# Up projection of a two-level (fp32 as high and low parts) encoder layer: activations' high and low parts side by side for 512 wide matmuls, and the last sum of weight quadrants by an accumulating DMA

## The chip, the cores and the metric

One core of a Trainium2 chip. The metric is the device time of one execution in microseconds (us), the median of three runs.

## The reference

One encoder layer on x of 512 tokens by 2048 channels, float32: a combined input projection, two token mixers, a merge, an output projection, a first layer norm, then the feed forward part and a second layer norm. The change touches the first product of the feed forward part:

```python
def conv_glu(x, w_up, conv_w, conv_b, w_down):
    u = x @ w_up                       # 512 x 2048 by 2048 x 11008
    gate, val = jnp.split(u, 2, axis=-1)
    a = jax.nn.gelu(dwconv_centred(gate, conv_w, conv_b), approximate=False)
    return (a * val) @ w_down
```

The convolution is over tokens, three taps per channel.

## The kernel before

Float32 accuracy is made from reduced-precision passes: each operand is split into a high part (rounded by ScalarE, `hi`) and the low rest (VectorE, `operand - high`), and a product is high by high, high by low and low by high, three matmuls that add up in the same PSUM bank.

The up projection runs in 43 steps (`FB`). A step makes 128 gate channels and the 128 val channels that go with them, for all 512 tokens, by Strassen's scheme in Winograd's form: the weight columns and rows make four quadrants of 1024 by 128 (gate or val columns, upper or lower half of the 2048 rows), the activations four of 1024 by 256 tokens, and seven products of 1024 by 128 by 256 replace eight. A step is therefore seven **blocks** (i = 0 to 6); `OPS` and `BANK` say which activation operand and which PSUM bank a block uses. The seven activation operands are made once, split, and stay in `aop`. A block is 8 slices of the contraction (`up_block`, L2267), each three matmuls of 256 columns by `add_three` (L2222): weight high by activation high (L2223), weight high by activation low (L2224), weight low by activation high (L2225).

Weights. SyncE loads the four quadrants of a step into `quad` (two sets, so a step ahead; L479, four transfers of 512 KB), each when the quadrant of two steps before has been split for the last time. Blocks 0, 3 and 5 use quadrants as loaded; the others use sums: block 1 takes q12 + q11, made by an accumulating DMA of GpSimd that adds q11's bytes from HBM to the loaded q12 (`add_b11`, L651, counted by `t1_in`); block 2 takes that + q22 (`form(step, 1)`, VectorE, L1528); block 4 takes q11 - that (`form(step, 2)`, L1532); block 6 takes block 2's sum + q21 (`form(step, 3)`, L1535). Each operand is then split: `operand_hi` (ScalarE, L989), which waits until the block three before is done, since `uw` has three buffers, and `operand_lo` (VectorE, L1553). The block waits for `op_lo`.

Results of a step. Between the blocks ScalarE copies PSUM banks: `seed` (L1070; bank of block 0 into the bank of blocks 2, 4, 6), `p5_copy` (L1075), `u2_copy` (L1080), and `gate_half` twice (L1093 copies the gate, L1094 makes the middle tap of the convolution with its bias). VectorE makes `c22` (L1721) and `c12` (L1726), each 128 x 256 from a PSUM bank and a copy, the outer taps in `conv` (L1731, L1732), and `product` (L1746) after ScalarE's `gelu` (L1099). Block 6 waits for `c22_done`, because `c22` frees the bank that it writes. All these act on [128, 256] halves of the tokens, or on [128, 512].

Every second step two products are combined and split for the down projection (`sums`, `ah_hi`, `ah_lo` L1758) and SyncE stores them with one transfer of 1792 KB (`spill`, L484) behind the four quadrant loads of that step. In 32 of the steps GpSimd also stores one chunk of the layer norm's output and loads the next (`store_chunk` L670, `load_chunk` L664); VectorE scales it in two parts (`residual`, L1772 in slot i = 3 and L1775 in slot i = 6).

Every engine's order is written out by hand: for each step and each i a fixed list (ScalarE from L1114, VectorE from L1777, GpSimd from L672, TensorE from L2281). An engine that waits holds up everything behind it. On GpSimd the order per step is: wait for a scaled chunk, store it, wait for the store, load the next chunk, wait for a loaded q12, `add_b11`.

"Step" below is one of the 43, "block" one of its seven products.

## Time and profile before

| | |
|---|---|
| three runs | 2813.02, 2815.32, 2814.93 us; median 2814.93 |
| the profiled execution's own time | 2812.55 us |
| its span, first to last instruction | 2810.5 us |
| mean granted TensorE clock | 0.988 |
| busy share of the span: TensorE, its weight loads, VectorE, ScalarE, GpSimd | 97%, 86%, 66%, 45%, 8% |
| first and last weight load of the up projection's matmuls | 1477.3 us, 2361.7 us |

A busy time sums durations of instructions; matmuls are pipelined, so their durations overlap and the distance between two starts is what a matmul costs in a dense stretch. "To landing" is from a DMA's issue to its last completion. A timeline row has start, duration, engine, line, and in brackets the idle time before it and what ended that.

### The profile page before, as it was taken

The page shows a single profiled execution, that of the slowest core. Times are in us where ns is not written, and L with a number is a line of the kernel's source. Part 1 is how long each engine was busy: PE and PEld are TensorE (multiplying, and loading weights), DVE is VectorE, ACT ScalarE, POOL GpSimd, SP SyncE. Part 2 cuts the span into 40 slices and gives each one's busy share as a digit, 9 for nine tenths or more (in the row PEclk, how much of TensorE's full clock was granted, in tenths as well). Part 3 has the DMA queues.
Part 4 walks back from the last instruction along what each step waited for, and adds up shares of the span by engine and source line. Part 5 has one row for each costly group of instructions (what it writes and reads, how often), then busy time and mean ns, then how long its engine had stood idle before and what let it go on. Part 6 is the DMA issues. An engine that isn't in the chain of part 4 may idle for free.

```text
span 2810.5 us, 42096 instructions
## 1 busy us (share of the span) xinstructions
PE 2737.0 (97%) x15963; PEld 2418.1 (86%) x15963; DVE 1844.4 (66%) x2452; ACT 1256.2 (45%) x1833; POOL 227.8 (8%) x298
## 2 busy tenths in 40 slices
PE   8999999999999999999979999999999999999995
PEld 7788888888888888888868999999999999888884
DVE  4465454555443333337897888888888876778788
ACT  4444444443333222224455555555555554444444
POOL 2000001110100000001010111111111101000000
PEclk9999999999999999999989999999999999999998
DMA  4333333332334444448535677767776768357452
GB/s 153 94 88 85 90 90 95 80 88 74 90 86 124 123 139 130 123 123 329 196 112 137 187 174 204 196 179 191 205 187 172 193 183 325 144 206 262 157 184 87
DMA packets 473748, 427.37 MB, mean 152 GB/s; under 512 B 16008, under 2 KB 417724, under 8 KB 469376
## 3 DMA queue, kind: packets, MB, share of 16 engines
q1 hardware_dynamic: 400672, 302.03, 35.1%
q0 software_dynamic: 70144, 119.04, 16.2%
q10 hardware_dynamic: 2784, 4.26, 0.4%
q8 instruction: 101, 1.65, 0.2%
q14 instruction: 47, 0.39, 0.0%
HBM read 361.28 MB, written 64.01 MB: 151 GB/s over the span
## 4 chain that ended last, share of the span: by engine, by line
PE 88%; DVE 8%; DMA 2%; issue 1%; ACT 1%; ACTq 0%; DVEq 0%
PE ps L2223 15%; PE ps L2224 14%; PE ps L2225 14%; PE ps L1961 14%; PE ps L1963 14%; PE ps L1962 14%; PE ps L1955 1%; DVE uw L1553 1%; PE ps L2171 1%; ACT uw L989 1%; DMA racc<-h_dram 1%; DVE aop L1706 1%; PE ps L2151 0%; DMA x_tok<-in_x 0%; DMA hx<-hn_dram 0%
## 5 line engine op out<-in xcount | busy, mean ns | idle before, releaser
L1185 DVE TENSOR_TENSOR wlo<-raw,whi 128x512 fp32r<-128x512 f32 x416 | 286.6, 691 | 629.2 <-ACT whi L724 626.3
L2223 PE MATMUL ps<-aop,uw 128*128 128x256 f32 x2408 | 685.1, 285 | 9.2 <-DVE aop L1706 6.2
L2224 PE MATMUL ps<-aop,uw 128*128 128x256 f32 x2408 | 683.1, 284 | 0.0
L2225 PE MATMUL ps<-aop,uw 128*128 128x256 f32 x2408 | 682.9, 284 | 0.0
L724 ACT ACTIVATE whi<-raw 128x512 fp32r<-128x512 f32 x416 | 260.7, 630 | 729.3 <-PE ps L1963 728.6
L1961 PE MATMUL ps<-xt_hi,whi 128*128 128x512 f32 x1408 | 553.2, 393 | 1.7 <-DVE wlo L1185 1.7
L1963 PE MATMUL ps<-xt_hi,wlo 128*128 128x512 f32 x1408 | 549.2, 390 | 0.0
L1962 PE MATMUL ps<-xt_lo,whi 128*128 128x512 f32 x1408 | 548.8, 390 | 0.0
L2223 PEld LDWEIGHTS ps<-aop,uw 128*128 128x128 f32 x2408 | 463.9, 193 | 13.0 <-DVE aop L1706 6.9
L2224 PEld LDWEIGHTS ps<-aop,uw 128*128 128x128 f32 x2408 | 464.0, 193 | 0.0
L2225 PEld LDWEIGHTS ps<-aop,uw 128*128 128x128 f32 x2408 | 463.9, 193 | 0.0
L1553 DVE TENSOR_TENSOR uw<-quad,uw 128x1024 fp32r<-128x1024 f32 x301 | 367.6, 1221 | 141.1 <-ACT uw L989 140.1
L989 ACT ACTIVATE uw<-quad 128x1024 fp32r<-128x1024 f32 x301 | 318.1, 1057 | 231.2 <-DVE quad L1535 138.9
L1961 PEld LDWEIGHTS ps<-xt_hi,whi 128*128 128x128 f32 x1408 | 264.7, 188 | 57.7 <-DVE wlo L1185 2.1
L1963 PEld LDWEIGHTS ps<-xt_hi,wlo 128*128 128x128 f32 x1408 | 264.6, 188 | 55.7
L1962 PEld LDWEIGHTS ps<-xt_lo,whi 128*128 128x128 f32 x1408 | 264.8, 188 | 53.3
L989 ACT ACTIVATE dw<-region 128x1024 fp32r<-128x1024 f32 x168 | 154.3, 919 | 218.1 <-PE ps L2225 202.8
L1553 DVE TENSOR_TENSOR dw<-region,dw 128x1024 fp32r<-128x1024 f32 x168 | 173.0, 1042 | 72.0 <-ACT dw L989 71.9
L2223 PE MATMUL ps<-dw,aopb 128*128 128x512 f32 x560 | 218.0, 389 | 1.7 <-DVE dw L1553 1.2
L2224 PE MATMUL ps<-dw,aopb 128*128 128x512 f32 x560 | 217.9, 389 | 0.0
L2225 PE MATMUL ps<-dw,aopb 128*128 128x512 f32 x560 | 217.8, 389 | 0.0
L2223 PEld LDWEIGHTS ps<-dw,aopb 128*128 128x128 f32 x560 | 105.1, 188 | 24.3 <-DVE dw L1553 1.6
(287 smaller groups left out, 3455.5 us busy)
## 6 DMA issues: line engine op xcount, KB each, us to landing
raw<-in_w_in SPq DMA_DIRECT2D x352, 256.0 KB, 2.7
quad<-in_ffn_w_up SPq DMA_DIRECT2D x172, 512.0 KB, 3.9
region<-in_ffn_w_down SPq DMA_DIRECT2D x32, 1280.0 KB, 9.1
a_dram<-ah SPq DMA_DIRECT2D x20, 1792.0 KB, 9.6
aopb<-a_dram POOLq DMA_DIRECT2D x28, 1280.0 KB, 8.1
quad<-in_ffn_w_up POOLq DMA_DIRECT2D x43, 512.0 KB, 6.6
w_region<-in_w_out SPq DMA_DIRECT2D x16, 1024.0 KB, 8.0
m_dram<-mh POOLq DMA_DIRECT2D x8, 1792.0 KB, 6.8
```

The lines of the kernel that those rows point to most:

```text
L724: nc.scalar.activation(whi[:, k % HL, :], raw[:, k % RAW, :], ACT.Copy).then_inc(w_hi_ready, 1)
L989: nc.scalar.activation(dst, src, ACT.Copy).then_inc(s["op_hi"], 1)
L1185: nc.vector.tensor_tensor(wlo[:, k % HL, :], raw[:, k % RAW, :], whi[:, k % HL, :].bitcast(F32), ALU.subtract).then_inc(w_lo_ready, 1)
L1553: nc.vector.tensor_tensor(w[:, 1, :, :], src, w[:, 0, :, :].bitcast(F32), ALU.subtract).then_inc(s["op_lo"], 1)
L1706: nc.vector.tensor_tensor(aop[:, :, 1, k, :], hs[k % 3][:, 0:7, :], aop[:, :, 0, k, :].bitcast(F32), ALU.subtract).then_inc(s["a_lo_done"], 1)
L1955: return nc.tensor.transpose(o, i, ident[0:rows, 0:rows])
L1961: mm(o, a_hi, b_hi, start=first, stop=False)
L1962: mm(o, a_hi, b_lo, start=False, stop=False)
L1963: return mm(o, a_lo, b_hi, start=False, stop=last)
L2223: mm(o, a_hi, b_hi, start=first, stop=False, skip_group_check=True)
L2224: mm(o, a_hi, b_lo, start=False, stop=False, skip_group_check=True)
L2225: return mm(o, a_lo, b_hi, start=False, stop=last, skip_group_check=True)
```

## The change

Three things. In `aop` the high and low parts of each slice stand side by side, and `up_block` multiplies the weight's high part by both in one matmul of 512 columns, then (before it, except in the first slice) the weight's low part by the high part in one of 256. The columns 0 to 255 of a bank then hold two of the three terms and 256 to 511 the third, so every PSUM operation works on 512 columns instead of 256, and the two halves are added at the end: `gate_low`, `gate_sum`, `conv_middle` replace `gate_half`, and `val_sum` adds up what `c22` and `c12` leave in the wider `p5c` and `u2c`. Third, `form(step, 3)` is gone: GpSimd adds q21 to `quad[...][1]` by a second accumulating DMA (`add_b21`), issued after block 2's operand is split and `form(step, 2)` is done, behind the next step's `add_b11` in GpSimd's order. `form(step, 2)` moves from slot i = 3 to slot i = 2. Left out below: two places where the counts of `p5_added` in the down projection shift.

```diff
@@ -88,7 +88,7 @@
 T_W = 8 * W_STEPS
-T_UP = T_W + 3 * FB
+T_UP = T_W + 2 * FB
@@ -230,14 +230,14 @@
         uw = sb("uw", [P, 3, 2, 8, P], 0, F32R)
-        aop = sb("aop", [P, 7, 2, 8, 256], 32 * K, F32R)
+        aop = sb("aop", [P, 7, 8, 2, 256], 32 * K, F32R)
         hs = [sb(f"hs{n}", [P, 8, 256], at * K) for n, at in enumerate((24, 160, 8))]
...
         ft = sb("ft", [P, S], 198 * K)
-        p5c = sb("p5c", [P, 256], 200 * K)
-        u2c = sb("u2c", [P, 256], 201 * K + 512)
+        p5u2 = sb("p5u2", [P, 1920], 200 * K)
+        p5c, u2c = p5u2[:, 0:512], p5u2[:, 1408:1920]
@@ -326,6 +326,11 @@
             return sum(r in held for held in REGIONS[:step + 1])
+        def p5u2_part(part):
+            head = p5u2[:, 256 * part:256 * part + 1]
+            return bass.AP(head.tensor, head.offset + 1408, [list(head.ap[0]), [-1408, 2], [1, 256]])
@@ -651,6 +656,13 @@
+            def add_b21(step):
+                pool.wait_ge(s["op_lo"], N_W + 7 * step + 3)
+                pool.wait_ge(s["t_formed"], T_W + 2 * step + 2)
+                pool.dma_start(quad[step % 2][1][:, :, :], wup[:, 8:16, step * P:(step + 1) * P],
+                               accum_op=ALU.add).then_inc(t1_in[step % 2], 16)
@@ -672,15 +684,20 @@
             load_chunk(0)
-            for step in range(2, 5):
-                add_b11(step)
+            for step in range(4):
+                if step:
+                    add_b11(step + 1)
+                add_b21(step)
             for c in range(32):
...
                 add_b11(c + 5)
+                add_b21(c + 4)
             for step in range(37, FB):
                 add_b11(step)
+                add_b21(step - 1)
+            add_b21(FB - 1)
@@ -957,10 +974,10 @@
                     else:
-                        if i == 1:
-                            act.wait_ge(t1_in[step % 2], 16 * (step // 2 + 1))
+                        if i in (1, 6):
+                            act.wait_ge(t1_in[step % 2], 16 * (2 * (step // 2) + 1 + (i == 6)))
                         else:
-                            act.wait_ge(s["t_formed"], T_W + 3 * step + {2: 1, 4: 2, 6: 3}[i])
+                            act.wait_ge(s["t_formed"], T_W + 2 * step + i // 2)
@@ -1004,7 +1021,7 @@
                 act.wait_ge(s["s_formed"], 8 + k + 1)
-                nc.scalar.activation(aop[:, :, 0, k, :], hs[k % 3][:, 0:7, :], ACT.Copy).then_inc(s["a_hi_done"], 1)
+                nc.scalar.activation(aop[:, :, k, 0, :], hs[k % 3][:, 0:7, :], ACT.Copy).then_inc(s["a_hi_done"], 1)
@@ -1065,34 +1082,39 @@
                 if step >= 2:
-                    act.wait_ge(s["c22_done"], W_STEPS + step - 1)
+                    act.wait_ge(s["c21_done"], W_STEPS + step - 1)
                 b0 = 3 * (step % 2)
-                nc.scalar.activation(ps[:, b0 + 1, 0:256], ps[:, b0, 0:256], ACT.Copy).then_inc(s["seed_done"], 1)
+                nc.scalar.activation(ps[:, b0 + 1, :], ps[:, b0, :], ACT.Copy).then_inc(s["seed_done"], 1)
             def p5_copy(step):
                 act.wait_ge(s["op_used"], N_W + 7 * step + 2)
-                act.wait_ge(s["c22_done"], W_STEPS + step)
-                nc.scalar.activation(p5c[:, :], ps[:, 3 * (step % 2) + 2, 0:256], ACT.Copy).then_inc(s["p5_copied"], 1)
+                act.wait_ge(s["p5_added"], W_STEPS + step)
+                if step == 0:
+                    act.wait_ge(s["ht_ps"], KB)
+                nc.scalar.activation(p5c, ps[:, 3 * (step % 2) + 2, :], ACT.Copy).then_inc(s["p5_copied"], 1)
             def u2_copy(step):
                 act.wait_ge(s["op_used"], N_W + 7 * step + 3)
-                act.wait_ge(s["c12_done"], W_STEPS + step)
-                nc.scalar.activation(u2c[:, :], ps[:, 3 * (step % 2) + 1, 0:256], ACT.Copy).then_inc(s["u2_copied"], 1)
-            def gate_half(step, half):
-                bank = 3 * (step % 2) + half
-                ts = slice(256 * half, 256 * half + 256)
-                if half == 0:
-                    act.wait_ge(s["op_used"], N_W + 7 * step + 4)
-                    if step == 0:
-                        act.wait_ge(s["hn_out"], 16 * 8)
+                act.wait_ge(s["p5_added"], W_STEPS + step)
+                nc.scalar.activation(u2c, ps[:, 3 * (step % 2) + 1, :], ACT.Copy).then_inc(s["u2_copied"], 1)
+            def gate_low(step):
+                act.wait_ge(s["op_used"], N_W + 7 * step + 7)
+                act.wait_ge(s["conv_done"], step)
+                b0 = 3 * (step % 2)
+                nc.scalar.activation(gate[:, :].rearrange("p (a t) -> p a t", a=2), ps[:, b0:b0 + 2, 256:512],
+                                     ACT.Copy).then_inc(s["c11_done"], 1)
+            def conv_middle(step):
+                act.wait_ge(s["c21_done"], W_STEPS + step + 1)
+                if step == 0:
+                    act.wait_ge(s["hn_out"], 16 * 8)
+                else:
                     act.wait_ge(s["mul_done"], step)
-                else:
-                    act.wait_ge(s["op_used"], N_W + 7 * step + 7)
-                nc.scalar.activation(gate[:, ts], ps[:, bank, 0:256], ACT.Copy)
-                nc.scalar.activation(ft[:, ts], ps[:, bank, 0:256], ACT.Identity, scale=par[:, PAR_FW + FB + step:PAR_FW + FB + step + 1],
-                                     bias=par[:, PAR_FB + step:PAR_FB + step + 1]).then_inc(s[("c11_done", "c21_done")[half]], 1)
+                nc.scalar.activation(ft[:, :], gate[:, :], ACT.Identity, scale=par[:, PAR_FW + FB + step:PAR_FW + FB + step + 1],
+                                     bias=par[:, PAR_FB + step:PAR_FB + step + 1]).then_inc(s["conv_a"], 1)
@@ -1120,21 +1142,22 @@
                     if i == 2 and step:
-                        gate_half(step - 1, 1)
+                        gate_low(step - 1)
                     if 7 * step + i >= 3:
                         operand_hi(N_W + 7 * step + i)
-                    if i == 3 and step:
+                    if i == 2 and step:
+                        conv_middle(step - 1)
+                    if i == 4 and step:
                         gelu(step - 1)
                     if i == 1 and step >= 3 and step % 2 and step < LEFT + 2:
                         ah_hi((step - 3) // 2)
-                    if i == 6:
-                        gate_half(step, 0)
                     if step == FB - 1 and i >= 5:
...
             operand_hi(N_UP + 1)
-            gate_half(FB - 1, 1)
+            gate_low(FB - 1)
             operand_hi(N_UP + 2)
+            conv_middle(FB - 1)
...
@@ -1524,15 +1547,12 @@
                     quad_ready(step, 3)
-                    dve.wait_ge(t1_in[step % 2], 16 * (step // 2 + 1))
+                    dve.wait_ge(t1_in[step % 2], 16 * (2 * (step // 2) + 1))
                     ins = nc.vector.tensor_tensor(q12[:, :, :], q12[:, :, :], q22[:, :, :], ALU.add)
-                elif j == 2:
+                else:
                     quad_ready(step, 0)
-                    dve.wait_ge(s["t_formed"], T_W + 3 * step + 1)
+                    dve.wait_ge(s["t_formed"], T_W + 2 * step + 1)
                     ins = nc.vector.tensor_tensor(q11[:, :, :], q11[:, :, :], q12[:, :, :], ALU.subtract)
-                else:
-                    quad_ready(step, 2)
-                    ins = nc.vector.tensor_tensor(q12[:, :, :], q12[:, :, :], q21[:, :, :], ALU.add)
@@ -1703,7 +1723,7 @@
                 dve.wait_ge(s["a_hi_done"], 8 + k + 1)
-                nc.vector.tensor_tensor(aop[:, :, 1, k, :], hs[k % 3][:, 0:7, :], aop[:, :, 0, k, :].bitcast(F32),
+                nc.vector.tensor_tensor(aop[:, :, k, 1, :], hs[k % 3][:, 0:7, :], aop[:, :, k, 0, :].bitcast(F32),
@@ -1718,33 +1738,48 @@
                 dve.wait_ge(s["op_used"], N_W + 7 * step + 5)
-                nc.vector.tensor_tensor(val[:, 256:512], p5c[:, :], ps[:, 3 * (step % 2) + 1, 0:256], ALU.subtract).then_inc(s["c22_done"], 1)
+                nc.vector.tensor_tensor(p5c, p5c, ps[:, 3 * (step % 2) + 1, :], ALU.subtract).then_inc(s["c22_done"], 1)
             def c12(step):
                 dve.wait_ge(s["u2_copied"], W_STEPS + step + 1)
                 dve.wait_ge(s["op_used"], N_W + 7 * step + 6)
-                nc.vector.tensor_tensor(val[:, 0:256], ps[:, 3 * (step % 2) + 2, 0:256], u2c[:, :], ALU.subtract).then_inc(s["c12_done"], 1)
+                nc.vector.tensor_tensor(u2c, ps[:, 3 * (step % 2) + 2, :], u2c, ALU.subtract).then_inc(s["c12_done"], 1)
+            def halves(tile):
+                return tile[:, :].rearrange("p (a t) -> p a t", a=2)
+            def gate_sum(step):
+                dve.wait_ge(s["c11_done"], W_STEPS + step + 1)
+                b0 = 3 * (step % 2)
+                nc.vector.tensor_tensor(halves(gate), halves(gate), ps[:, b0:b0 + 2, 0:256], ALU.add).then_inc(s["c21_done"], 1)
+            def val_sum(step):
+                dve.wait_ge(s["c22_done"], W_STEPS + step + 1)
+                dve.wait_ge(s["c12_done"], W_STEPS + step + 1)
+                if step:
+                    dve.wait_ge(s["mul_done"], step)
+                nc.vector.tensor_tensor(halves(val), p5u2_part(0), p5u2_part(1), ALU.add).then_inc(s["p5_added"], 1)
             def conv(step):
-                dve.wait_ge(s["c21_done"], W_STEPS + step + 1)
+                dve.wait_ge(s["conv_a"], 4 * ML_H + step + 1)
                 w0, w2 = par[:, PAR_FW + step:PAR_FW + step + 1], par[:, PAR_FW + 2 * FB + step:PAR_FW + 2 * FB + step + 1]
...
                 dve.wait_ge(s["gelu_done"], step + 1)
-                dve.wait_ge(s["c22_done"], W_STEPS + step + 1)
-                dve.wait_ge(s["c12_done"], W_STEPS + step + 1)
+                dve.wait_ge(s["p5_added"], W_STEPS + step + 1)
                 if step == FB - 1:
-                    dst = x_raw[:, :].rearrange("p (a t) -> p a t", a=2)
+                    dst = halves(x_raw)
                 elif step % 2:
...
                     dst = ab[:, 2:8:5, :]
-                nc.vector.tensor_tensor(dst, val[:, :].rearrange("p (a t) -> p a t", a=2), ft[:, :].rearrange("p (a t) -> p a t", a=2),
-                                        ALU.mult).then_inc(s["mul_done"], 1)
+                nc.vector.tensor_tensor(dst, halves(val), halves(ft), ALU.mult).then_inc(s["mul_done"], 1)
@@ -1780,14 +1815,18 @@
                         c12(step - 1)
+                    if i == 2 and step:
+                        gate_sum(step - 1)
+                    if 7 * step + i >= 3:
+                        operand_lo(N_W + 7 * step + i)
+                    if i == 2 and step:
+                        val_sum(step - 1)
+                    if i in (1, 2) and step + i > 1:
+                        form(step, i)
+                    if i == 3 and step:
+                        conv(step - 1)
                     if i == 5 and step:
                         product(step - 1)
-                    if 7 * step + i >= 3:
-                        operand_lo(N_W + 7 * step + i)
-                    if i in (1, 3, 5) and step + i > 1:
-                        form(step, (0, 1, 3, 5).index(i))
-                    if i == 2 and step:
-                        conv(step - 1)
@@ -1800,6 +1839,8 @@
             operand_lo(N_UP + 1)
+            gate_sum(FB - 1)
+            val_sum(FB - 1)
...
@@ -2267,8 +2308,14 @@
                 step, i = divmod(n - N_W, 7)
-                return add_three(ps[:, 3 * (step % 2) + BANK[i], 0:256], uw[:, n % 3, 0, k, :], uw[:, n % 3, 1, k, :],
-                                 aop[:, OPS[i], 0, k, :], aop[:, OPS[i], 1, k, :], i < 2 and k == 0, k == 7)
+                bank, first = 3 * (step % 2) + BANK[i], i < 2 and k == 0
+                both, high = aop[:, OPS[i], k, :, :].rearrange("p h t -> p (h t)"), aop[:, OPS[i], k, 0, :]
+                if not first:
+                    mm(ps[:, bank, 0:256], uw[:, n % 3, 1, k, :], high, start=False, stop=False, skip_group_check=True)
+                last = mm(ps[:, bank, :], uw[:, n % 3, 0, k, :], both, start=first, stop=k == 7, skip_group_check=True)
+                if first:
+                    last = mm(ps[:, bank, 0:256], uw[:, n % 3, 1, k, :], high, start=False, stop=False, skip_group_check=True)
+                return last
@@ -2285,7 +2332,7 @@
                     if i == 0 and step >= 2:
-                        pe.wait_ge(s["c11_done"], W_STEPS + step - 1)
+                        pe.wait_ge(s["c21_done"], W_STEPS + step - 1)
                     elif i == 1 and step >= 2:
                         pe.wait_ge(s["c12_done"], W_STEPS + step - 1)
                     elif i == 2:
```

## Rows read from the trace of the kernel before

**Rows 1.** Page, busy time of each engine
```profile
PE 2737.0 (97%) x15963; PEld 2418.1 (86%) x15963; DVE 1844.4 (66%) x2452; ACT 1256.2 (45%) x1833; POOL 227.8 (8%) x298
```

**Rows 2.** Windows: us, busy us (instructions) of PE, PEld, DVE, ACT, POOL, clock, DMA share, GB/s
```profile
1477.00:2362.00 885.00, 875.80 (x7227) 871.97 (x7226) 721.31 (x801) 488.64 (x673) 119.58 (x132) 0.99 0.72 188
1900.00:2000.00 100.00, 99.77 (x830) 99.42 (x829) 82.09 (x95) 55.84 (x78) 14.66 (x17) 1.00 0.75 190
```

**Rows 3.** Timeline of PE in the up projection, two starts 24 matmuls apart
```profile
1803.11 0.28 PE L2225 MATMUL ps<-aop,uw 128*128 128x256 f32 x1
...
1805.99 0.28 PE L2225 MATMUL ps<-aop,uw 128*128 128x256 f32 x1
```

**Rows 4.** Timeline of PE in the input projection, two starts 12 matmuls apart
```profile
300.22 0.39 PE L1961 MATMUL ps<-xt_hi,whi 128*128 128x512 f32 x1
...
302.94 0.39 PE L1961 MATMUL ps<-xt_hi,whi 128*128 128x512 f32 x1
```

**Rows 5.** Waits from 1600 to 2300 us: in total, times, longest
```profile
ACT uw L989 <- DVE quad L1535: 116.4, 34, 4.8
...
PE ps L2223 <- DVE val L1721: 1.4, 4, 0.6
```

**Rows 6.** Groups by form, whole span: line, operation, shapes, count, busy us, mean ns
```profile
L1535 DVE TENSOR_TENSOR quad<-quad,quad 128x1024 f32<-128x1024 f32 x43 | 52.4, 1218 | 0.0
L1473 DVE TENSOR_TENSOR mt<-ps,mg 128x512 f32<-128x512 f32 x16 | 10.9, 684 | 3.0 <-PE ps L1963 3.0
L1758 DVE TENSOR_TENSOR ah<-ab,ah 128x1792 fp32r<-128x1792 f32 x20 | 40.4, 2018 | 0.0
L1094 ACT ACTIVATE ft<-ps,par 128x256 f32<-128x256 f32 x86 | 48.1, 559 | 0.0
L1099 ACT ACTIVATE ft<-ft 128x512 f32<-128x512 f32 x43 | 27.2, 633 | 17.6 <-DVE ft L1732 17.6
```

**Rows 7.** Timeline of ACT: gate_half, seed, block 6's high part; gate_half of step 38
```profile
1813.86 0.38 ACT L1093 ACTIVATE gate<-ps 128x256 f32<-128x256 f32 x1 [2.12 <-PE ps L2225]
...
1816.74 0.37 ACT L1070 ACTIVATE ps<-ps 128x256 f32<-128x256 f32 x1 [1.09 <-PE ps L2225]
...
1826.26 1.06 ACT L989 ACTIVATE uw<-quad 128x1024 fp32r<-128x1024 f32 x1 [2.43 <-DVE quad L1535]
...
2261.24 0.38 ACT L1093 ACTIVATE gate<-ps 128x256 f32<-128x256 f32 x1 [1.77 <-PE ps L2225]
```

**Rows 8.** Timeline of DVE in the first step of rows 7: block 6's low part, then residual and c22
```profile
1827.35 1.22 DVE L1553 TENSOR_TENSOR uw<-quad,uw 128x1024 fp32r<-128x1024 f32 x1 [1.13 <-ACT uw L989]
1828.50 0.42 DVE L1775 TENSOR_TENSOR hx<-hx,bx 128x256 f32<-128x256 f32 x1
1828.83 0.41 DVE L1721 TENSOR_TENSOR val<-p5c,ps 128x256 f32<-128x256 f32 x1
```

**Rows 9.** Timeline of POOL: add_b11 in that step, in the next, and in step 38
```profile
1816.10 1.63 POOL L651 DMA_DIRECT2D quad<-in_ffn_w_up  x1
...
1835.00 1.59 POOL L651 DMA_DIRECT2D quad<-in_ffn_w_up  x1 [0.17 <-issue]
...
2261.64 1.54 POOL L651 DMA_DIRECT2D quad<-in_ffn_w_up  x1 [20.66 <-DMA quad<-in_ffn_w_up]
```

**Rows 10.** Landing of those three, from the source view of L651 in windows around each
```profile
DMA to landing us min/median/max: 8.8/8.8/8.8
...
DMA to landing us min/median/max: 6.4/6.4/6.4
...
DMA to landing us min/median/max: 9.8/9.8/9.8
```

**Rows 11.** Windows of 1 us at step 38 (columns as in rows 2): the store, then the accumulation
```profile
2264.00:2265.00 1.00, 1.00 (x10) 1.00 (x9) 0.96 (x3) 0.88 (x2) 0.00 (x0) 1.00 1.00 430
...
2267.00:2268.00 1.00, 1.00 (x10) 1.00 (x9) 1.00 (x1) 0.38 (x1) 0.00 (x0) 1.00 1.43 200
```

**Rows 12.** DMA issues from 1600 to 2200 us, the store: KB, median us to landing
```profile
a_dram<-ah SPq DMA_DIRECT2D x15, 1792.0 KB, 9.7
```

6 lines of the change are left out of this document (3 added, 3 removed).

## The prediction

> **What bounds the kernel now.** I read the page first: TensorE is busy 97% of the span [rows 1]. Then windows over the stage that changes: in its 885 us TensorE holds 7,227 matmuls and VectorE is busy 82%; in 100 us from its middle TensorE starts 830 [rows 2]. The timeline gives the price of one: 24 matmuls of 256 columns start in 1805.99 - 1803.11 = 2.88 us, 0.1200 each [rows 3]. 830 x 0.12 = 99.6 of 100 us, so this stage is bound by TensorE's issue, with almost no wait in it. A step is 168 x 0.12 = 20.16 us, a block 2.88. The waits say the same from the other side: in 700 us TensorE waited 1.4 us for c22 in four places, while ScalarE waited 116.4 us for block 6's last sum without harm [rows 5]. Block 6 is where the chain beside TensorE is closest to it.
>
> **Matmuls.** In the input projection 12 matmuls of 512 columns start in 2.72 us, 0.2267 each [rows 4]. The second 256 columns cost 0.1067, so each matmul carries 0.0133 us that does not depend on its width. A slice was 3 x 0.1200 = 0.3600 and becomes 0.1200 + 0.2267 = 0.3467. With 43 x 7 x 8 = 2,408 slices: **-32.1 us**. A 256 wide matmul beside a 512 wide one is in no row. Bounds for what a slice saves: nothing, if the 0.0133 stays with the weight load of each term, and 0.0133; I take 0.0133, since both widths give the same remainder. The first step's two blocks run while activations are still being split and gain nothing: 16 x 0.0133 = 0.2, left out. A step becomes 19.41 us, a block 2.773.
>
> The Trainium skill ("TensorE: Matmul & The Clock Gate", section "Back-to-back issue gap") gives a warm gap of N/2.4 + 2.5 ns, so only 2.5 ns independent of width. Here rows show 13.3 at both widths; by that rule the saving would be 2,408 x 2.5 ns = 6.0 us.
>
> **VectorE.** Per step it loses one sum of quadrants, 1.22, gains gate_sum and val_sum, and c22 and c12 grow from 0.41 [rows 8] to some 0.68 (a 512 wide sum from PSUM, L1473): -1.22 + 2 x 0.68 + 2 x 0.27 = +0.68 us [rows 6]. It was busy 82.09 of 100 us [rows 2], 16.5 of 20.16; now 17.2 of 19.41, 89%. Odd steps also hold the sums and the low part for the store (2.02 [rows 6]; 0.68 + 0.41 + 0.41 by their sizes), so an odd step has about 19.0 of 19.41 and an even one 15.4. It fits in the mean, and a delay in an odd step is worked off only in the next even one. Cost if nothing else is late: 0.
>
> **ScalarE.** seed, p5_copy and u2_copy grow by some 0.26 each (0.63 at 512 against 0.37), gate_half twice (2 x (0.38 + 0.56) = 1.88) becomes 0.63 + 0.82 = 1.45: +0.35 us on 56 of 100 busy [rows 2, 6, 7]. No cost. conv_middle stands ahead of seed and waits for gate_sum, but is done some 2.5 us after the step starts, and seed cannot start before 2.77.
>
> **The last sum.** This is where the time can go back. Count from T, when ScalarE learns that the step before is done (1813.86 [rows 7]). Before, block 6's high part began at T + 12.4 in that step and its low part ended at 1828.57, T + 14.7, c22 at T + 15.4 [rows 7, 8]; block 6 is due at T + 17.1, six blocks less the 0.16 by which a matmul outlasts its issue (0.28 - 0.12). Now it is due at 6 x 2.773 - 0.16 = T + 16.5.
>
> The new chain to add_b21: gate_low 0.63, high part of block 2 1.06, its low part 1.22, val_sum 0.68, form(step, 2) 1.22: T + 4.8 [rows 6 to 8]. GpSimd is free then: add_b11 was issued at T + 2.2 and took 1.63 [rows 9]. An accumulation of this size lands 6.4 us after its issue when nothing is in its way [rows 10], so T + 11.3. Then high part 1.06, low part 1.22, residual 0.42, c22 0.68, in VectorE's order: 3.4, T + 14.7. That is early by 1.8 us: alone, add_b21 is free.
>
> It is not alone. In every even step a 1792 KB store of the step before is on its way and takes 9.7 us to land [rows 12]. The add_b11 issued then lands after 8.8 or 9.8 instead of 6.4 [rows 10]: while the store runs the engines move 430 GB/s, and only after it comes the accumulation, at 1.43 busy share and 200 GB/s [rows 11]. So transfers issued earlier are served first, and an accumulation of 512 KB holds the engines for some 3.3 us (its bytes by 160 to 200 GB/s). add_b21 uses the same queue behind add_b11:
> - even steps with a chunk (16): add_b11 lands at T + 2.2 + 8.8 = T + 11.0, add_b21 at T + 14.3, block 6 ready at T + 17.7 instead of 16.5: 1.2 late. In the shorter step the chunk and the store also come somewhat earlier against T; I take 1.0.
> - odd steps with a chunk (16): add_b11 (1835.00, T + 1.0) lands at T + 7.4 and is out of the way. But VectorE comes out of a late even step into its full odd one, so form(step, 2) ends 1.5 to 2 later and add_b21 lands at T + 13.0: + 3.4 is 16.4, at the limit. I take 0.2.
> - the last 8 steps have no chunks: in step 38 (T = 2261.24) add_b11 lands at T + 0.4 + 9.8 = 10.2 [rows 7, 9, 10], add_b21 at 13.6, no residual in the way, 16.6: 0.1 late in the even ones, nothing in total. Steps 0 to 2 have no store: nothing.
>
> Sum: 16 x 1.0 + 16 x 0.2 = +19 us. GpSimd's own 43 x 1.6 us of issue costs nothing, it is busy 15%.
>
> **Total.** -32 + 19 = **-13 us**. The profiled execution took 2812.55, 2.4 below the median and 2.1 above its span: 2799.6 on its terms, 2802 against the median of 2814.9. A comparison here can tell about 0.2%, 5.6 us, from no change.
>
> **Rivals.**
> (A) The forecast, -6 to -22: a saving of 32 of which a late block 6 takes back a part, chiefly in even steps. Chance 0.42.
> (B) No stall: add_b21 lands in time everywhere, because the shorter step moves store and chunk forward or two accumulations overlap. For it: 1.2 us decides, less than the 2.4 to 3.4 us by which landings differ. Against: the same queue. -32, 2783. Chance 0.20.
> (C) Slower: block 6's last sum paces every step. Place: between form(step, 2) and block 6's high part. The step's own quadrant load (q11 of two steps later, 512 KB, issued after block 4's low part, near T + 9) runs before or between add_b21's packets. At 430 GB/s such a load holds the engines 1.2 us [rows 11]. With half of it in the way, stalls are 1.6, 0.8 and 0.6 (even, odd, last 8): 16 x 1.6 + 16 x 0.8 + 8 x 0.6 = +43, net +11, 2826; with all of it +24 more, 2850. It decides from a mean stall of 0.75 us a step, what the matmuls save. For it: odd steps have no reserve on VectorE, so a delay is carried on. Against: landings in rows 10 suggest order of arrival, and add_b21 arrives first. Chance 0.25.
> (D) The fixed 0.0133 doesn't shrink with the number of matmuls, or the gain and the stalls just meet: -5 to +5, 2815. Chance 0.13, of which a small part is the mix of widths.
>
> The Trainium skill ("DMA: Bandwidth & Descriptors", section "Issuing engines are not separate DMA queues") says that transfers of all issuing engines end up on the same 16 DMA engines and interleave. This speaks for (C). The trace here agrees that they share, but shows the accumulation waiting for the store rather than mixed with it.
>
> **Numbers.** Faster by over 0.2%: 0.42 and 0.20; within: 0.13; slower: 0.25. Range: from (B)'s 2782 to 2835, which takes in (C) with half a load and a little more in the way and leaves its far end out. The forecast's own range is 2793 to 2809.
>
> **What would show it.** Starts in the up projection 0.1200 and 0.2267 after each other, 0.3467 a slice; if the pair takes 0.36, the first term is wrong. The time from add_b21's issue to landing: some 6.4 in odd steps, 8 to 9.5 in even ones. TensorE's waits in the stage: about 19 us in all, ended by c22 or by block 6's low part, the former above all, larger in even steps. If instead the waits end at block 0 to 5 by VectorE's low parts, VectorE is the bound and my budget is wrong. If ScalarE waits for form(step, 2) or gate_sum beyond a microsecond and seed comes late, the moved slots cost what I put at nothing. A step of 19.41 us throughout would be (B), one over 20.16 us (C).

## The result and the profile after

| | before | after |
|---|---|---|
| median of 20 runs each, us | 2813.74 (2809.59 to 2818.63) | 2819.48 (2813.23 to 2828.93) |
| span of the profiled execution, us | 2810.5 | 2818.6 |

The ratio is 1.0022, with a 95% interval of 1.0015 to 1.0029: slower by 0.2%, where 13 us less were forecast. Below, "after" is the changed kernel, a ratio is against the runs of before that stood beside the run in question, and a difference in us from after is between two medians.

The page of after: busy time of each engine, the chain's shares, the two groups of the up projection's matmuls (L2314 is weight low by activation high, 256 columns; L2315 weight high by both parts, 512), and two DMA issues (count, KB, median us to landing).

```profile
PE 2721.0 (97%) x13555; PEld 2287.6 (81%) x13555; DVE 1865.4 (66%) x2495; ACT 1267.7 (45%) x1747; POOL 296.1 (11%) x341
...
PE 72%; DVE 12%; DMA 9%; issue 4%; ACT 3%; POOL 0%; ACTq 0%; DVEq 0%; POOLq 0%
...
L2315 PE MATMUL ps<-aop,uw 128*128 128x512 f32 x2408 | 846.5, 399 | 0.0
...
L2314 PE MATMUL ps<-aop,uw 128*128 128x256 f32 x2322 | 655.7, 282 | 22.8 <-DVE p5u L1741 16.3
...
quad<-in_ffn_w_up POOLq DMA_DIRECT2D x86, 512.0 KB, 6.9
...
a_dram<-ah SPq DMA_DIRECT2D x20, 1792.0 KB, 10.7
```

TensorE has 2,408 fewer matmuls than before [rows 1], as the diff says, and a new row of idle time ended by `c22` (L1741). The chain has 9% of DMA, where it had 2% before. The middle of the stage, in windows (columns as in rows 2):

```profile
1900.00:2000.00 100.00, 96.36 (x544) 82.83 (x544) 81.33 (x97) 55.00 (x65) 21.16 (x21) 1.00 0.91 208
```

TensorE, at 99.77 before [rows 2], is now idle for 3.6 of 100 us. Nothing else is full: VectorE has 81.33, ScalarE 55.00. The DMA engines' share rose from 0.75 to 0.91. The waits from 1600 to 2300 us (total, times, longest), which answer to rows 5:

```profile
ACT uw L1006 <- DMA quad<-in_ffn_w_up: 114.4, 34, 5.8
...
PEld ps L2314 <- issue: 25.2, 29, 2.6
...
PE ps L2314 <- DVE p5u L1741: 16.1, 24, 2.3
```

Both waits of TensorE's side are at block 6. From the starts of the first matmuls of all blocks, what blocks 5 and 6 of a step last beyond its blocks 2 to 4 adds up to 25 us for the stage: 1.2 in a mean even step with a chunk (0.3 to 3.7), 0.4 in such an odd one, nothing in the last eight. Before, the same count gives 7 us, 0.35 in most odd steps.

**The stage against the rest.** ScalarE's `seed` runs once a step, so its first and last start measure 42 steps. Before, then after:

```profile
1491.94 0.37 ACT L1070 ACTIVATE ps<-ps 128x256 f32<-128x256 f32 x1 [4.37 <-PE ps L2225]
...
2345.12 0.37 ACT L1070 ACTIVATE ps<-ps 128x256 f32<-128x256 f32 x1 [1.09 <-PE ps L2225]
```
```profile
1490.25 0.58 ACT L1087 ACTIVATE ps<-ps 128x512 f32<-128x512 f32 x1 [4.38 <-PE ps L2315]
...
2341.43 0.58 ACT L1087 ACTIVATE ps<-ps 128x512 f32<-128x512 f32 x1 [0.29 <-PE ps L2315]
```

42 steps took 853.2 and take 851.2 us: the stage is 2.0 faster. But from the last seed to the end of the span it was 465.4 (2810.5 - 2345.1) and is 477.2: 11.8 slower. The spans' 8.1 us are therefore: start of the stage -1.7 (it differs by 3.4 us between after and e14, which are alike up to there), stage -2.0, tail +11.8. In the stage, the 25 us of waits leave 826 us of matmuls, 19.67 a step, against 846 and 20.15: -20, and +18 of waits.

**The tail.** The waits of after and of before from 2325 to 2460 us have one pair of rows that differs. After:

```profile
DVE racc L1859 <- DMA racc<-h_dram: 12.1, 1, 12.1
PEld ps L2002 <- issue: 11.9, 1, 11.9
PE ps L2002 <- DVE racc L1859: 11.5, 1, 11.5
```

Before:

```profile
DVE racc L1818 <- DMA racc<-h_dram: 2.4, 1, 2.4
...
PE ps L1961 <- DVE racc L1818: 1.9, 1, 1.9
```

These are the first matmuls that need a PSUM bank back after the up projection: VectorE must first add pieces of the residual (`racc`) that GpSimd loads. Its timeline in the last step of after:

```profile
2343.96 1.54 POOL L663 DMA_DIRECT2D quad<-in_ffn_w_up  x1 [16.75 <-DVE quad L1555]
2344.84 1.40 POOL L710 DMA_DIRECT2D racc<-h_dram  x1
2345.57 1.59 POOL L706 DMA_DIRECT2D aopb<-a_dram  x1
...
2355.82 0.75 POOL L710 DMA_DIRECT2D racc<-h_dram  x1 [1.96 <-PE ps L2315]
```

The same of before:

```profile
2345.68 0.74 POOL L693 DMA_DIRECT2D racc<-h_dram  x1 [23.49 <-PE ps L2225]
...
2359.79 0.75 POOL L693 DMA_DIRECT2D racc<-h_dram  x1 [1.84 <-PE ps L2225]
```

Step 42's `add_b21` (L663) waits 16.75 us for `form(42, 2)`, and the down projection's loads stand behind it. The first is issued 3.4 us after the step's seed, before it was 0.6 (2345.68 - 2345.12). Windows of after (columns as in rows 2) show the DMA engines idle, then slow on the accumulation, then full. In the last three rows TensorE waits and comes back, with a lower granted clock at first.

```profile
2344.00:2346.00 2.00, 2.00 (x13) 1.72 (x13) 1.96 (x4) 1.55 (x2) 2.00 (x3) 1.00 0.11 45
...
2348.00:2350.00 2.00, 2.00 (x13) 1.77 (x12) 1.35 (x2) 1.14 (x2) 1.66 (x2) 1.00 1.46 183
...
2376.00:2378.00 2.00, 0.00 (x0) 0.00 (x0) 0.00 (x0) 0.00 (x0) 0.00 (x0) 0.88 1.04 419
...
2388.00:2390.00 2.00, 2.00 (x6) 1.53 (x5) 1.49 (x2) 0.00 (x0) 0.00 (x0) 0.50 1.04 420
...
2392.00:2394.00 2.00, 2.00 (x10) 1.63 (x10) 0.00 (x0) 0.00 (x0) 0.00 (x0) 1.00 1.02 410
```

From 2354 to the wait's end the engines move 410 to 420 GB/s without a gap, so what they fell behind by they don't make up. VectorE waits for the fourth piece, the one issued at 2355.82. It is not issued late (14.4 us after the seed, 14.7 before); it lands late, because of what is in front of it. Its landing, after and then before:

```profile
DMA to landing us min/median/max: 27.8/27.8/27.8
```
```profile
DMA to landing us min/median/max: 18.2/18.2/18.2
```

That is at 2383.6, 42.2 us after the seed instead of 32.8, and VectorE starts at 2383.74. The second piece lands 5.8 us later against the seed than before, the third and the fourth 9.4. Between the second and the third SyncE's first load of down projection weights goes by: issued 11.5 us after the seed, it lands at 25.9, as before (25.6), but now ahead of the third piece (30.8) and not behind it (21.4).

### The profile page after: what moved, and what is told of

Same layout as the page of the kernel before. It is cut to its first block, busy times and chain, and to the rows that moved or that the text cites. A ratio compares the mean times of both kernels' runs of the same rounds, so it can differ in the third digit from the quotient of the medians.

```text
span 2818.6 us, 37389 instructions
## 1 busy us (share of the span) xinstructions
PE 2721.0 (97%) x13555; PEld 2287.6 (81%) x13555; DVE 1865.4 (66%) x2495; ACT 1267.7 (45%) x1747; POOL 296.1 (11%) x341
## 4 chain that ended last, share of the span: by engine, by line
PE 72%; DVE 12%; DMA 9%; issue 4%; ACT 3%; POOL 0%; ACTq 0%; DVEq 0%; POOLq 0%
PE ps L2002 14%; PE ps L2004 14%; PE ps L2003 14%; DMA quad<-in_ffn_w_up 8%; PE ps L2315 7%; PE ps L2264 6%; PE ps L2265 6%; PE ps L2266 6%; PE ps L2314 3%; ACT uw L1006 2%; DVE uw L1573 2%; PE ps L1996 1%; DVE quad L1551 1%; DVE quad L1555 1%; DMA racc<-h_dram 1%
## 5 line engine op out<-in xcount | busy, mean ns | idle before, releaser
L2315 PE MATMUL ps<-aop,uw 128*128 128x512 f32 x2408 | 846.5, 399 | 0.0
L2314 PE MATMUL ps<-aop,uw 128*128 128x256 f32 x2322 | 655.7, 282 | 22.8 <-DVE p5u L1741 16.3
L2315 PEld LDWEIGHTS ps<-aop,uw 128*128 128x128 f32 x2408 | 449.7, 189 | 101.2
L2314 PEld LDWEIGHTS ps<-aop,uw 128*128 128x128 f32 x2322 | 440.7, 190 | 37.0 <-issue 26.3
L2264 PEld LDWEIGHTS ps<-dw,aopb 128*128 128x128 f32 x560 | 105.2, 188 | 24.3 <-DVE dw L1573 1.6
L2265 PEld LDWEIGHTS ps<-dw,aopb 128*128 128x128 f32 x560 | 105.2, 188 | 21.7
L2266 PEld LDWEIGHTS ps<-dw,aopb 128*128 128x128 f32 x560 | 105.2, 188 | 21.7
```

Source lines behind the costliest of these rows:

```text
L2264: mm(o, a_hi, b_hi, start=first, stop=False, skip_group_check=True)
L2265: mm(o, a_hi, b_lo, start=False, stop=False, skip_group_check=True)
L2266: return mm(o, a_lo, b_hi, start=False, stop=last, skip_group_check=True)
L2314: mm(ps[:, bank, 0:256], uw[:, n % 3, 1, k, :], high, start=False, stop=False, skip_group_check=True)
L2315: last = mm(ps[:, bank, :], uw[:, n % 3, 0, k, :], both, start=first, stop=k == 7, skip_group_check=True)
```

## The experiments

The runs up to e13 were planned with the stage alone in view; e14 to e16 ask about the tail. The first set takes one part at a time.

**e1: no add_b21.** On after; it leaves q21 out of block 6's operand.
```diff
-                add_b21(step)
...
-                        if i in (1, 6):
+                        if i == 1:
```


> The changed kernel without the second accumulating DMA: block 6 uses block 2's sum, so q21 is missing from it; that part of the computation is left out. Theory S (block 6's last sum lands late: about 28 us of TensorE waits at block 6 in steps 4 to 34, in the even steps most): the waits go, the time falls to 2785 to 2797, and block 6 lasts as long as the others. Theory V (VectorE's and ScalarE's longer operations and moved slots pace the step): the waits stay, at some block, and the time stays over 2805. Theory P (a pair of matmuls costs 0.3467 us at first and 0.353 later in the stage, in two levels): with no waits, the slice keeps one level; if the upper level comes from the waits, the step is 19.41 us throughout and the time is near 2782; if from something else, 19.75 us and near 2795.

Measured 2785.56, ratio 0.9899 (0.9882 to 0.9916). TensorE never waits. The seeds of two steps apart:
```profile
1608.21 0.58 ACT L1082 ACTIVATE ps<-ps 128x512 f32<-128x512 f32 x1 [0.30 <-PE ps L2310]
1627.98 0.58 ACT L1082 ACTIVATE ps<-ps 128x512 f32<-128x512 f32 x1
```
19.77 and 19.71 in turn, a mean of 19.74, to the end of the stage (828.4 us): a slice costs 19.74/56 = 0.3525, not 0.3467, with nothing late. With the last sum left out altogether, the rest of the change is worth 27 us; part of that is VectorE's relief from the sum, and e3 tells what the layout is worth with the sum on VectorE.

**e2: add_b21 alone.** Before, with the last sum by the second accumulation, matmuls 256 wide.
```diff
+                add_b21(c + 4)
...
-                    ins = nc.vector.tensor_tensor(q12[:, :, :], q12[:, :, :], q21[:, :, :], ALU.add)
```


> The kernel before with the accumulating DMA for the last sum alone: matmuls stay 256 wide, the step 20.16 us, form(step, 2) in slot 2, form(step, 3) gone. Theory S: block 6 is due 0.6 us later than in the changed kernel, so only even steps are late, by 0 to 2 us; against the kernel before, whose odd steps lose 0.35 us each at block 6, the time comes out between -5 and +15 us. Theory V: VectorE has 1.2 us less in each step and nothing more, so it is faster by 5 to 7 us.

Measured 2815.64, ratio 1.0010 (1.0001 to 1.0019); one of its eleven executions took 6513.07 us, far outside the others' 2811.66 to 2821.47, and nothing rests on it. At first I read this as "about nothing". Its stage is 847.3 us, 5.9 shorter than before (the waits of odd steps are gone), and its tail 472.7, 7.3 longer: two effects of opposite sign.

**e3: 512 wide alone.** After, with the last sum on VectorE in slot i = 5.
```diff
+                    ins = nc.vector.tensor_tensor(q12[:, :, :], q12[:, :, :], q21[:, :, :], ALU.add)
...
-                    if i in (1, 2) and step + i > 1:
+                    if i in (1, 2, 5) and step + i > 1:
```


> The changed kernel with the last sum made by VectorE again (slot 5), no second accumulating DMA; the 512 wide matmuls and all that goes with them stay. VectorE then has 18.4 us of work in a step of 19.4 to 19.8, 20.2 in odd ones. Theory S: the waits of even steps go; what is left are waits of odd steps by VectorE; time 2790 to 2805. Theory V: no faster than the changed kernel, 2815 to 2830.

Measured 2794.26, ratio 0.9934 (0.9922 to 0.9947). The waits from 1600 to 2300 us:
```profile
PEld ps L2313 <- issue: 9.6, 15, 0.6
...
PE ps L2313 <- DVE p5u L1740: 5.3, 15, 0.4
```
Small and regular: each odd step up to 33 loses some 0.55 us at block 6, released by VectorE; in such a step VectorE has the sums and low part for the store as well. The tail is 465.7, as before.

**e4: the store later.** After; SyncE waits for `add_b21` of the odd step before it stores.
```diff
                 if step >= 5 and step % 2:
+                    sp.wait_ge(t1_in[0], 16 * (step + 1))
                     spill((step - 5) // 2)
```


> The changed kernel with one wait more on SyncE: the 1792 KB store of the odd step is issued only when the next step's second accumulating DMA has landed. Theory S, in the form that the store holds up add_b11 and with it add_b21: in even steps add_b21 lands 6.4 to 7.5 us after its issue instead of 8 to 10, the waits at block 6 fall from 28 us to under 12, time 2800 to 2808. Rival, that add_b21 is late by its own issue time and by add_b11 in front of it whatever the store does: landing stays over 8 us, time within 4 us of the changed kernel.

Measured 2876.19, ratio 1.0237 (1.0224 to 1.0250). Even steps came out nearly clean (in steps 6, 8 and 10 `add_b21` lands after 6.7 to 7.0 us), but the quadrants' loads are queued behind the waiting SyncE: in step 7 q12 came late, `add_b11` was issued 4.6 us after the seed, `add_b21` right behind it and landed after 10.4, and the step took 27.7 us. A miss as a cure, but it shows that without the store ahead of them both accumulations land earlier (the `add_b11` in front of steps 6, 8 and 10 after 8.2, 6.9 and 6.7 us).

**e5: add_b21 first.** After, with the two calls swapped on GpSimd.
```diff
-                add_b11(c + 5)
                 add_b21(c + 4)
+                add_b11(c + 5)
```


> The changed kernel with add_b21 of a step ahead of the next step's add_b11 on GpSimd, nothing else. Theory S, sharpened by the run with the late store (even steps clean, odd steps late because their add_b11 was late): what makes add_b21 late is the add_b11 in front of it. Then in even steps add_b21 waits for the store alone, lands 6.5 to 8 us after its issue instead of 8 to 10, and the waits at block 6 fall under 12 us: 2797 to 2806. Rival, the store itself is what add_b21 waits for: landing stays at 8 to 9, time within 5 us of the changed kernel's 2819. A new wait can appear at block 1 of the next step, since add_b11 is issued 3 to 4 us later.

Measured 2803.43, ratio 0.9971 (0.9961 to 0.9981), 16 us less than after, with a stage of 832.1 and a tail of 474.3. Landings of `add_b21` (L663), from the source view of 1600 to 2200 us, first after, then e5:
```profile
DMA to landing us min/median/max: 6.5/8.0/10.2
```
```profile
DMA to landing us min/median/max: 6.4/6.6/7.2
...
DMA to landing us min/median/max: 8.8/10.4/12.2
```
The last line is `add_b11` of e5, issued 0.9 us behind. Now it is the one that is late: the two run one after the other. `add_b21`'s landing no longer depends on the store at all, in even and odd steps alike. So what held it in even steps of after was not the store itself but `add_b11`, which had waited for the store.

**e7: order within a slice.** After, with the 512 wide matmul ahead of the 256 wide in all slices.
```diff
+                mm(ps[:, bank, :], uw[:, n % 3, 0, k, :], both, start=first, stop=False, skip_group_check=True)
+                return mm(ps[:, bank, 0:256], uw[:, n % 3, 1, k, :], high, start=False, stop=k == 7, skip_group_check=True)
```


> The changed kernel with the 512 wide matmul ahead of the 256 wide one in every slice. The run without the second accumulation had no wait at block 6 and yet 19.74 us a step in every step, 0.3525 us a slice; in other runs 0.3475 appears for a few steps after a long wait. Theory P1, the extra 0.005 to 0.006 us comes from which weight load meets which matmul: the other order changes the level, block times of 2.77 or over 2.85 throughout. Theory P2, it belongs to each change between the widths: block times 2.77 to 2.83 as before. Time within 6 us of the changed kernel either way, since waits at block 6 take up the difference.

Measured 2815.45, ratio 1.0005 (0.9996 to 1.0014). The same two levels of a block, 2.77 and 2.83 us, and waits of the same size (23 us by the same count). Order is not the cause of the two levels.

**e8: 256 wide in the new layout.** After, with the pair of a slice as three matmuls.
```diff
+                    mm(ps[:, bank, 0:256], uw[:, n % 3, 0, k, :], high, start=False, stop=False, skip_group_check=True)
+                    last = mm(ps[:, bank, 256:512], uw[:, n % 3, 0, k, :], aop[:, OPS[i], k, 1, :], start=False, stop=k == 7, skip_group_check=True)
```


> The changed kernel with the same three terms in the same 512 wide banks, but three matmuls of 256 columns instead of a 256 and a 512 wide one (but for the first slices of blocks 0 and 1). It tells what the width alone brings. Theory: slice 0.3600, step 20.16 us; block 6 is due 0.4 us later than in the changed kernel, so waits fall from 28 to some 15 us and the time is 2822 to 2832. If the width brings nothing behind the waits: 2819, as the changed kernel.

Measured 2819.01, ratio 1.0026 (1.0015 to 1.0038): as slow as after. Its undisturbed step is 20.15 against 19.74, yet the stage takes 848.8 us against 851.2, with 2 us of waits instead of 25. In after, the time saved by wide matmuls was all given back: block 6 is ready when its last sum is, however fast TensorE gets there.

**e9: mixed.** After, but even steps (where the store runs) sum on VectorE and odd ones by `add_b21`.
```diff
             def add_b21(step):
+                if step % 2 == 0:
+                    return
...
-                    if i in (1, 2) and step + i > 1:
-                        form(step, i)
+                    if (i in (1, 2) or i == 5 and step % 2 == 0) and step + i > 1:
+                        form(step, min(i, 3))
```


> The changed kernel, but even steps make the last sum on VectorE (slot 5) and only odd steps by the second accumulating DMA. Even steps have VectorE time to spare and the store in the way; odd steps have a full VectorE and no store. Theory S with the VectorE budget: no waits at block 6 in even steps, under 0.3 us in odd ones (the run with all sums on VectorE loses 0.55 us in each odd step, 9 us in all); 2783 to 2789, below the 2794 of that run. Rival, odd steps are late by the landing in any case: 2790 or more.

Measured 2789.14, ratio 0.9920 (0.9906 to 0.9933). Each resource is used in the steps in which it has room: no wait of TensorE in the stage, 828.4 us as in e1, with the whole product made. A window of it:
```profile
1900.00:2000.00 100.00, 100.00 (x569) 86.83 (x568) 90.96 (x106) 58.93 (x69) 19.51 (x20) 1.00 0.86 204
```
VectorE is 91% busy and TensorE waits for nothing, so a VectorE at 81% was not after's bound.

**e11: both of these.** e9 with `add_b21` ahead of `add_b11`.


> The version in which even steps sum on VectorE and odd ones by add_b21, with add_b21 ahead of add_b11 on GpSimd. If block 6 is never late in the mixed version, its order has nothing left to give: 2789 us, the same within 0.1%. If its odd steps still lose something behind add_b11, 1 to 3 us less. If add_b11 (for the next step's block 1) becomes late behind add_b21 in odd steps, waits appear at block 1 and it is slower, 2790 to 2800.

Measured 2791.52, ratio 0.9918 (0.9903 to 0.9933): no gain, and an interval nearly that of e9. The profiled stage is 833.6 instead of 828.4, with a few waits at block 6 and one at block 1. With the store out of `add_b21`'s way, nothing is gained by moving it ahead of `add_b11`.

**Where the slice's time went.** e10 is e1 with the weight's low part multiplied by both halves too (it leaves q21 out as well), so that all matmuls have 512 columns.
```diff
-                    mm(ps[:, bank, 0:256], uw[:, n % 3, 1, k, :], high, start=False, stop=False, skip_group_check=True)
+                    mm(ps[:, bank, :], uw[:, n % 3, 1, k, :], both, start=False, stop=False, skip_group_check=True)
```


> The kernel after without add_b21 (q21 is left out of block 6), and the weight's low part is also multiplied by both parts, so a slice is two matmuls of 512 columns and no width changes within a block. Theory 1, the missing 0.006 us of a slice belongs to the alternation of widths: two starts take 2 x 0.2267 = 0.4533 throughout, a block 3.627, a step 25.39 us in every step, one level only. Theory 2, 512 columns are slower in this stage than in the input projection (memory reads or weight loads beside everything else): above 0.2267 each, a block 3.65 to 3.70, and two levels as before. Nothing waits at block 6 in either case, the step has 5 us of slack.

One run, 3025.1 us. Two starts of one line, 16 matmuls apart:
```profile
1899.80 0.39 PE L2309 MATMUL ps<-aop,uw 128*128 128x512 f32 x1
...
1903.43 0.39 PE L2309 MATMUL ps<-aop,uw 128*128 128x512 f32 x1
```
3.63/16 = 0.2269, and steps of 25.39 throughout, which is 112 x 0.2267. So 512 columns cost no more in this stage than in the input projection [rows 4]; the missing 0.0058 us of a slice comes with two widths in turn. In after both prices occur. Starts of the 512 wide matmuls, in step 2 and in step 38:
```profile
1530.10 0.39 PE L2315 MATMUL ps<-aop,uw 128*128 128x512 f32 x1
...
1531.48 0.39 PE L2315 MATMUL ps<-aop,uw 128*128 128x512 f32 x1
...
2264.85 0.40 PE L2315 MATMUL ps<-aop,uw 128*128 128x512 f32 x1
...
2266.26 0.40 PE L2315 MATMUL ps<-aop,uw 128*128 128x512 f32 x1
```
Four slices in 1.38 and in 1.41 us.

**e12 and e13: widths apart.** e9 and after, with eight 512 wide matmuls and then eight 256 wide ones in each block.
```diff
-                    for k in range(8):
-                        last = up_block(n, k)
+                    for part in range(2):
+                        for k in range(8):
+                            last = up_block(n, k, part)
```


> The mixed version with the two widths of a block apart: eight matmuls of 512 columns, then eight of 256, so that the width changes twice in a block instead of 16 times. Theory 1, the missing 0.006 us of a slice comes with the alternation (two matmuls of 512 columns in a slice took 0.4533 throughout in the run before): blocks 2.77 to 2.79, a step 19.4 to 19.5, at most 42 x 0.33 = 14 us less than the mixed version's 2789, about 2776; waits may take a part back, since VectorE has less room. Theory 2, it belongs to 256 wide matmuls fed beside wide ones in this layout whatever their order: 19.74 again, 2789.

Measured 2779.56, ratio 0.9879 (0.9864 to 0.9894), 9.6 us less than e9. Two blocks' starts of PE's timeline:
```profile
1901.49 2.00 PE L2324 MATMUL ps<-aop,uw 128*128 128x512 f32 x8
1903.33 1.12 PE L2326 MATMUL ps<-aop,uw 128*128 128x256 f32 x8
1904.28 2.00 PE L2324 MATMUL ps<-aop,uw 128*128 128x512 f32 x8
```
A block is 2.79 us, a mean step 19.55, a little over the 19.4 to 19.5 expected: of the 0.33 us that a step of 19.74 has over 19.41, grouping gets back 0.19.

> The kernel after with the two widths of a block apart, eight matmuls of 512 columns and then eight of 256. The last sum is still made behind add_b11, so block 6 cannot start earlier than it does. Theory: a block saved 0.05 us, but block 6 of the steps with a store waits that much longer, as it did when the matmuls were narrow; the same as the kernel after within 0.2%, 2815 to 2821. If the grouping were worth its full 14 us here, 2805.

Measured 2813.10, ratio 1.0003 (0.9994 to 1.0012), 6.4 less than after: more than the none that I expected, less than the 14.

**The tail.** e14 is after with step 42's last sum on VectorE, and nothing else.
```diff
-            add_b21(FB - 1)
...
-                        if i in (1, 6):
+                        if i == 1 or i == 6 and step < FB - 1:
```


> The kernel after, except that in the last step (42) alone the last sum is made by VectorE, so that GpSimd has no add_b21 in front of the loads with which the down projection begins. In the kernel after TensorE stands still 11.5 us once, at the first matmuls behind the up projection, where VectorE waits 12.1 us for the residual's pieces (racc); before it was 1.9 and 2.4. Theory: this one transfer, at the head of a queue of loads that keeps the DMA engines full from there on, costs 9 to 10 us of the 2819.5: here TensorE's wait is 2 to 3 us and the time 2810 (2808 to 2812), a little under the kernel before, with the up projection itself unchanged. Rival: the pieces are late because the up projection ends earlier against a fixed backlog of loads; then the wait stays at 8 to 12 us and the time at 2818 to 2820.

Measured **2807.11**, ratio 0.9976 (0.9966 to 0.9986). The stage is 848.1 us, the tail 464.6; its waits from 2325 to 2460 us:
```profile
DVE racc L1862 <- DMA racc<-h_dram: 2.1, 1, 2.1
...
PE ps L2005 <- DVE racc L1862: 1.6, 1, 1.6
```
The up projection ends as early as in after, so the rival (a fixed backlog) falls. One of 43 transfers cost 12.4 us (2819.48 - 2807.11) and decided the sign: without it the change is 0.24% faster than before. That is more than the 9 to 10 us that I expected: the wait alone is 9.9 us less, and the clock behind it gives back another 2.4 (last section).

**e15: grouped, and the same edit.**


> Both: the widths of a block apart (512 eight times, then 256 eight times) and step 42's last sum on VectorE, the other 42 steps by add_b21. The grouped kernel took 2813.1 and stood still 9.3 us at the same place. Theory: 7 us less, 2806 (2804 to 2808). Rival (a fixed backlog): 2813 again.

Measured 2805.46, ratio 0.9958 (0.9944 to 0.9971): 7.6 less than e13, as expected, with a wait of 2.4 us in the tail. All other kernels that keep step 42's `add_b21` wait there for 7.4 to 11.8 us (e2, e4, e5, e7, e8, e13); e1, e3, e9, e11 and e12 don't have it and wait 1.6 to 2.5.

**e16: before, GpSimd held.** No accumulation is added, only the wait in front of the down projection's loads.
```diff
             for step in range(37, FB):
                 add_b11(step)
+            pool.wait_ge(s["t_formed"], T_W + 3 * (FB - 1) + 2)
```


> The kernel before, with GpSimd made to wait for step 42's form(step, 2) before it issues the down projection's first loads, as it does in the kernel after, but with no accumulating transfer. The first piece is then issued some 4 us later. Theory, the place in GpSimd's order is what costs, all of its loads move by the delay: TensorE's wait there goes from 1.9 to 5 or 6 us, the time to 2817. If the accumulation's own time on the DMA engines is what costs (3.3 us at under 200 GB/s), a smaller part: 2 to 3 us of wait, 2814.

Measured 2820.21, ratio 1.0023 (1.0014 to 1.0032), 7.2 us slower with one wait added. The first load is issued 4.2 us after the seed instead of 0.6, and:
```profile
PE ps L1962 <- DVE racc L1819: 6.6, 1, 6.6
```
4.7 us more of wait for 3.6 of delay, and with the clock behind it more than either theory allowed (2817, 2814). In after the delay is 2.8 us (3.4 against 0.6); in the same proportion that is 3.7 of its extra 9.6 us of wait. So GpSimd's order is a part that costs by itself; the rest I put down to the accumulation in front of the loads, which no run tried alone. The landings fit: against before, e16's second piece lands 2.9 us later and its fourth 4.7, after's 5.8 and 9.4, in both 1.6 times as late once SyncE's loads have come in. Of after's 5.8 us at most 2.8 are the delay of the first issue; the other 3 are an estimate of what the accumulation's time on the engines costs, near the 3.3 of the prediction.

## Why the prediction was wrong

| term, us | forecast | measured |
|---|---|---|
| matmuls of the stage | -32 | -20 |
| waits at block 6 | +19 | +25 |
| waits of before that go | 0 | -7 |
| start of the stage | 0 | -2 |
| behind the stage | 0 | +12 |
| sum | -13 | +8 (spans; medians +6) |

**GpSimd, costed at nothing: the step that decided the sign.** I wrote that its issues cost nothing since it is busy 15%. That is a rate, for an engine whose order matters. In 42 steps the issues themselves cost nothing that shows. In the last one `add_b21(FB - 1)` is put in front of the loads that the down projection starts with, and from there the DMA engines are full (410 to 420 GB/s) until after TensorE's wait. The diff shows the line; I didn't ask what is queued behind it, nor read any row past the stage. e14 takes it away alone and gets 12.4 us back. None of my rivals has it.

**Matmuls: right mechanism, size too large.** 0.3467 occurs, in the first steps and now and then later, but 0.3525 is the usual price (e1: always). I had put the mix of widths among the unknowns, with bounds of 0 and 0.0133, and took the far end because both widths left the same remainder. The measured 0.0075 lies in the middle, and makes 18 us of the 20 over 42 steps; the few steps at 0.3467 make the rest. The starts of e10 keep to 0.2267 and those of [rows 3] to 0.1200, so what doesn't depend on the width is 13.3 ns where the width doesn't change. The Trainium skill ("TensorE: Matmul & The Clock Gate", section "Back-to-back issue gap") has 2.5 ns there, for a matmul by itself, by which 6.0 us would have been saved; the trace doesn't agree, the stage's matmuls saved 20.

**The last sum: right place, a little small.** `form(step, 2)` ended at T + 4.9 in step 16 (4.8 forecast), and `add_b21` landed after 8.1 us there, at T + 13.6 against 14.3 forecast, and after 6.5 in step 17. Once the store runs, its landings were 6.5 to 7.2 us in odd steps and 7.1 to 10.2 in even ones. But I took one even step as the type; the mean even step loses 1.2, not 1.0: steps 18 and 22, with landings of 9.8 and 10.2, lose 3.7 and 2.5, and an early landing gives nothing back. A mean of waits is more than the wait at the mean. That step 18 loses more than step 22 is the clock: 1.6 of its 3.7 us are matmuls at 0.50 behind the wait (last section). Odd steps lost 0.4 instead of 0.2. And I took the 1.4 us of [rows 5] for all that before waited; the starts show 7 us, which a last sum off VectorE takes away (e2's stage is 5.9 shorter). For the queue: what stands in front of `add_b21` is `add_b11` (e5), as my sum had it: in e5 the two are issued 0.9 us apart and land some 4.7 apart, one after the other. The Trainium skill ("DMA: Bandwidth & Descriptors", section "Issuing engines are not separate DMA queues") says that transfers started by different engines interleave, which I let speak for (C). The tail of after agrees: SyncE's load, issued 2.8 us behind GpSimd's third piece, lands 4.8 us ahead of it. For two accumulations from one engine, of which the section says nothing, e5 shows one after the other.

**VectorE and ScalarE: right.** `c22`, `gate_sum` and `val_sum` take 0.68, `seed` 0.58, `gate_low` 0.59, `conv_middle` 0.80, and e9 has no wait with VectorE at 91%. On the page VectorE grew by 0.49 us a step (1844.4 to 1865.4) where I had 0.68. That an odd step is full shows where it does more (e3, 0.55 us a step).

**The rivals.** (C) had the sign and wasn't what happened: the mean wait in the stage is 25/42 = 0.60 us a step, under the 0.75 from which it decides. With the tail mended (e14) the change gains 5.9 us, just short of forecast (A), -6 to -22, and it comes that near partly by luck: the matmuls brought 12 us less than forecast and the waits took 6 more, but 7 us of waits of before went that I hadn't counted. Of "what would show it", the 0.3467, the landings, `c22` as the releaser and the larger waits in even steps were the right things to look at; a row on the seam behind the stage was missing.

## What to carry to other kernels

When an operation moves to another engine's queue, walk that queue to its end: look at the last instance in particular, at what is issued behind it, and whether the stage that begins there has spare DMA time. If the engines are full from there on, each microsecond of delay comes out again as idle time of the engine that waits last (here 4.7 us for 3.6, e16), and more through its clock. Compare two kernels stage by stage first, by an instruction that runs once a step: a difference of 8 us in the whole was here -2 in the stage that was changed and +12 behind it. And where two resources are each full in alternate steps, split the work by step: e9 and, with the widths grouped, e12 (2779.56, 1.2% under before) beat both kernels.
